# Seven block products for eight in the last up projection of a two-block transformer, with the weight sums on GpSimd

## The reference, cut to what matters

```
D_MODEL = 2048; SEQ = 256; D_FF_2 = 5632
h2 = rmsnorm(x, ffn_norm_g[i])
x = x + (jax.nn.silu(h2 @ w_ffn_gate[i]) * (h2 @ w_ffn_up[i])) @ w_ffn_down[i]
return rmsnorm(x, final_norm_g)
```

## Time and profile before

| | |
|---|---|
| median of 3 runs | 2800.74 us (2800.68 to 2802.15) |
| the profiled execution | 2802.66 us, its span 2800.8 us |
| PE busy | 2784.7 us, 99% of the span |
| VectorE, ScalarE, GpSimd busy | 1947.5, 1377.4, 167.3 us |
| granted TensorE clock, mean | 0.998 |

### The profile page before, as it was taken

One profiled execution on the slowest core, in us unless ns is written; L12 is line 12 of the kernel. 1 busy time (PEld: TensorE's weight loads), 2 busy tenths in 40 slices (PEclk: granted clock), 3 DMA queues, 4 the chain that ended last, 5 costly groups with the idle time before them and its releaser, 6 DMA issues.

```text
span 2800.8 us, 45274 instructions
## 1 busy us (share of the span) xinstructions
PE 2784.7 (99%) x15267; PEld 2385.4 (85%) x15267; DVE 1947.5 (70%) x2978; ACT 1377.4 (49%) x1865; POOL 167.3 (6%) x82
## 2 busy tenths in 40 slices
PE   9999999999999999999999999999999999999998
PEld 7888988888888888888888888888888888888887
DVE  6987787866885786788866777777655555555555
ACT  5336755544554455665544555554454444443444
POOL 6860010000000000000000000000000000000000
PEclk9999999999999999999999999999999999999999
DMA  8975365665665665655555655655666656656664
GB/s 227 260 181 136 92 181 180 192 205 188 188 192 191 187 193 186 186 149 160 154 190 177 181 170 173 182 173 180 196 203 189 190 190 195 188 188 195 189 191 154
DMA packets 510448, 512.69 MB, mean 183 GB/s; under 512 B 90014, under 2 KB 410366, under 8 KB 509822
## 3 DMA queue, kind: packets, MB, share of 16 engines
q1 hardware_dynamic: 510254, 511.19, 60.7%
q10 hardware_dynamic: 80, 0.01, 0.0%
HBM read 505.83 MB, written 5.24 MB: 182 GB/s over the span
## 4 chain that ended last, share of the span: by engine, by line
PE 97%; DVE 1%; SPq 1%; DMA 0%; POOL 0%; ACT 0%; issue 0%; ACTq 0%; DVEq 0%
PE banks L1936 32%; PE banks L1939 16%; PE banks L1968 12%; PE banks L1966 12%; PE banks L1967 12%; PE banks L1951 3%; PE banks L1912 2%; PE banks L1953 1%; SPq L433 1%; PE banks L1920 1%; PE banks L2207 1%; PE banks L1922 1%; PE banks L1921 1%; PE banks L2333 0%; PE banks L2383 0%; PE banks L2016 0%
## 5 line engine op out<-in xcount | busy, mean ns | idle before, releaser
L613 ACT ACTIVATE w_two<-w_raw 128x1024 fp32r<-128x1024 f32 x944 | 995.2, 1059 | 1135.9 <-PE banks L1968 555.1
L1090 DVE TENSOR_TENSOR w_two<-w_raw,w_two 128x1024 fp32r<-128x1024 f32 (+1 forms) x881 | 1075.6, 1229 | 655.3 <-ACT w_two L613 649.3
L1936 PE MATMUL banks<-hp,w_two 128*128 128x512 f32 x3200 | 1012.5, 397 | 1.8 <-issue 1.0
L1939 PEld LDWEIGHTS banks<-hp,w_two 128*128 128x128 f32 x3200 | 601.1, 188 | 140.6
L1939 PE MATMUL banks<-hp,w_two 128*128 128x256 f32 x3200 | 632.0, 278 | 0.0
L1936 PEld LDWEIGHTS banks<-hp,w_two 128*128 128x128 f32 x3200 | 489.3, 189 | 8.9 <-issue 5.1
L1966 PE MATMUL banks<-w_two,yp 128*128 128x512 f32 x1056 | 412.0, 390 | 0.0
L1968 PE MATMUL banks<-w_two,yp 128*128 128x512 f32 x1056 | 411.0, 389 | 0.0
L1967 PE MATMUL banks<-w_two,yp 128*128 128x512 f32 x1056 | 411.0, 389 | 0.0
L1968 PEld LDWEIGHTS banks<-w_two,yp 128*128 128x128 f32 x1056 | 198.2, 188 | 41.4
L1967 PEld LDWEIGHTS banks<-w_two,yp 128*128 128x128 f32 x1056 | 198.3, 188 | 40.6
(11 more groups left out here) (310 smaller groups left out, 2412.0 us busy)
## 6 DMA issues: line engine op xcount, KB each, us to landing
w_raw<-in_w_in SPq DMA_DIRECT2D x480, 256.0 KB, 3.1
w_raw<-in_w_up SPq DMA_DIRECT2D x352, 256.0 KB, 2.9
w_raw<-in_w_down SPq DMA_DIRECT2D x176, 256.0 KB, 3.0
w_raw<-in_w_ffn_gate SPq DMA_DIRECT2D x176, 256.0 KB, 2.8
w_raw<-in_w_ffn_up SPq DMA_DIRECT2D x176, 256.0 KB, 2.9
w_raw<-in_w_ffn_down SPq DMA_DIRECT2D x176, 256.0 KB, 3.3
w_raw<-in_w_out SPq DMA_DIRECT2D x128, 256.0 KB, 3.6
w_raw<-in_w_mla_proj SPq DMA_DIRECT2D x64, 256.0 KB, 3.0
```

What stands on the lines that cost most here:

```text
L613: nc.scalar.activation(w_hi[:, s, 0:n], w_raw[:, s, 0:n], ACT.Copy).then_inc(hi_ready, 1)
L1090: v.tensor_tensor(w_lo[:, s, 0:n], w_raw[:, s, 0:n], w_hi[:, s, 0:n].bitcast(f32), ALU.subtract)\
L1936: mm(banks[:, b, :], w_hi[:, s, at:at + P], rhs[:, k0 + k, :], start=k0 + k == kt_first, stop=False)
L1939: ins = mm(banks[:, b, 0:T], w_lo[:, s, at:at + P], rhs[:, k0 + k, 0:T], start=False, stop=k0 + k == kt_last)
```

## The change

The first step of the last up projection stays as it is (phase `up2_0`, now with one step). The other ten steps become three runs (`run0` to `run2`, of 3, 4 and 3 steps). In a run the input tiles are paired: tile k with tile k + 8. For the pairs 0 to 5 (`QUADS = 6`) the eight block products (two token blocks, two input halves, gate and up) are replaced by seven products of sums, a quad: with gate blocks G0, G1 and up blocks U0, U1 (0 and 1 the input halves), GpSimd forms T1 = U0 - G0, T2 = U1 - T1, T3 = U1 - U0, T4 = G1 - T2 (`sum_1` to `sum_4`), and the activations are used as four prepared sums S1 to S4 and as they are. Pairs 6 and 7 are done plainly (`plain`). A step has 7 x 6 + 8 = 50 operands (`OPS`), each one input tile by 512 columns, and PE does 6 x 7 x 3 + 8 x 2 x 3 = 174 matmuls of 512 columns. Every operand is split in hi by ScalarE (`op_high`) and in lo by VectorE (`op_low`), except four plain ones of each step, which GpSimd splits (`by_pool`). The seven results collect in seven banks; VectorE adds them together into gate and up (`plus`: eight adds a step, each from a bank and an SBUF operand), and ScalarE copies one. The gate and up products (`gate_products`, `mids`: four a step) now read SBUF alone. S1 to S4 are made once, by ten GpSimd adds and four GpSimd subtractions of 128x768 beside four ScalarE copies, while `up2_0` runs. Weights come in blocks of 128x512, as many bytes as before and one DMA of 256 KB each as before, into eleven raw places (three more in `cst`), with eight places for the split operands. The turning of a step's result (`mid_turn`) uses bank 7 and lies after quads 1 and 3 of the next step.

In NSA, unit 1 of `w_out_conv` no longer waits for unit 0 to be taken out, and VectorE does `lo("q", 0, 12)` between `scores(0)` and `scores(1)` rather than behind them.

```diff
+QUADS = 6
+PLAIN = [h + k for h in (0, KT // 2) for k in range(QUADS, KT // 2)]
+T1, T2, T3, B11, B21, B22, T4 = range(7)
+FIRST_PLAIN = 7 * QUADS
+OPS = FIRST_PLAIN + 2 * len(PLAIN)
+BLOCKS = 2 * KT
+RUNS = [(p, 1 if p == 0 else 0, k // 4) for p, (t, k) in enumerate(PARTS)]
+RUN_NAMES = [f"run{p}" for p in range(len(PARTS))]
+S_AT = (3, 5, 8, 10, 14)
+OP_SLOTS, RAW_SLOTS = 2 * R, 2 * R + 3
...
+def by_pool(n):
+    return n % OPS >= FIRST_PLAIN and n % 2 == 1
...
+            for r, (p, i0, i1) in enumerate(RUNS):
+                t0, n = PARTS[p]
+                for st in range(i1 - i0):
+                    cols = slice(t0 * P + (i0 + st) * WIDE, t0 * P + (i0 + st + 1) * WIDE)
+                    for m in range(BLOCKS):
+                        b = BLOCKS * st + m
+                        if m < 4 * QUADS:
+                            g, c = divmod(m, 4)
+                            w, k = (w_gate, w_up, w_up, w_gate)[c], g + c // 2 * (KT // 2)
+                        else:
+                            half, k = divmod(m - 4 * QUADS, len(PLAIN))
+                            w, k = (w_gate, w_up)[half], PLAIN[k]
+                        block_wait(r, b)
+                        sp.dma_start(raw_block(b), w[k * P:(k + 1) * P, cols]).then_inc(block_raw(b), 16)
...
+            def op_high(r, n):
+                src = block_of(n) if n % OPS >= FIRST_PLAIN or n % OPS % 7 in (B11, T3, B22, B21) else None
+                if n % OPS < FIRST_PLAIN and n % OPS % 7 in (T1, T2, T3, T4):
+                    act.wait_ge(sem("op_sums"), sums_made(r, n // OPS * QUADS + n % OPS // 7, n % OPS % 7))
+                else:
+                    act.wait_ge(block_raw(src), block_arrived(r, src))
+                if n >= OP_SLOTS:
+                    act.wait_ge(unit_used, U0[f"run{r}"] + n - OP_SLOTS + 1 + LEAD)
+                else:
+                    act.wait_ge(unit_used, U0[f"run{r}"] - R + n // 2 + 1 + LEAD)
+                nc.scalar.activation(op_hi(n), op_source(n), ACT.Copy).then_inc(hi_ready, 1)
...
+            v1, v2, v3, v4 = (s_f[j][:, :, P:] for j in range(4))
+            added.link(s_step(v1, act_part(0, 1, 0), act_part(1, 1, 0), ALU.add))
+            added.link(s_step(s_tmp, act_part(0, 1, 1), act_part(1, 1, 1), ALU.add))
+            added.link(s_step(v1, v1, s_tmp, ALU.add))
+            added.link(s_step(v2, v1, act_part(0, 0, 0), ALU.subtract))
+            added.link(s_step(v2, v2, act_part(0, 0, 1), ALU.subtract))
...
+            def sum_1(r, q):
+                first, second = came(r, q, 0), came(r, q, 1)
+                if q > 1:
+                    wait_low(pool, r, quad_op(q - 2, T1))
+                nc.gpsimd.tensor_tensor(t_first[:, q % 2, :], second, first, ALU.subtract).then_inc(sem("op_sums"), 1)
+            def sum_2(r, q):
+                last = came(r, q, 2)
+                pool.wait_ge(sem("op_sums"), sums_made(r, q, T1))
+                if q > 1:
+                    wait_low(pool, r, quad_op(q - 2, T4))
+                nc.gpsimd.tensor_tensor(t_other[:, q % 2, :], last, t_first[:, q % 2, :], ALU.subtract).then_inc(sem("op_sums"), 1)
+            def sum_3(r, q):
+                last, second = came(r, q, 2), raw_block(quad_block(q, 1))
+                nc.gpsimd.tensor_tensor(second, last, second, ALU.subtract).then_inc(sem("op_sums"), 1)
+            def sum_4(r, q):
+                third = came(r, q, 3)
+                wait_low(pool, r, quad_op(q, T2))
+                nc.gpsimd.tensor_tensor(t_other[:, q % 2, :], third, t_other[:, q % 2, :], ALU.subtract).then_inc(sem("op_sums"), 1)
+            def plain_low(r, n):
+                if by_pool(n):
+                    pool.wait_ge(hi_ready, U0[f"run{r}"] + n + 1)
+                    nc.gpsimd.tensor_tensor(op_lo(n), op_source(n), op_hi(n).bitcast(f32), ALU.subtract).then_inc(sem("op_low_pool"), 1)
...
+            lo("q", 0, 12)
             scores(1)
-            lo("q", 0, 12)
...
+            def op_low(r, n):
+                if not by_pool(n):
+                    dve.wait_ge(hi_ready, U0[f"run{r}"] + n + 1)
+                    v.tensor_tensor(op_lo(n), op_source(n), op_hi(n).bitcast(f32), ALU.subtract).then_inc(sem("op_low"), 1)
+            def plus(dst, a, bank):
+                return v.tensor_tensor(dst, banks[:, bank, :], a, ALU.add).then_inc(chunk_out, 1)
...
+                down, nu = f"down2_{p}", n // 2
+                r, (_, i0, i1) = p, RUNS[p]
+                for st in range(i1 - i0):
+                    gs, n0 = t0 // 4 + i0 + st, OPS * st
+                    for m in range(6 if st == 0 else 0, OPS):
+                        op_low(r, n0 + m)
+                        if st and m == 2:
+                            gate_sums(r, n0 - len(PLAIN) - 1)
+                        if st and m == 4:
+                            gate_products(gs - 1)
+                        if st and m == 6:
+                            up_sums(gs - 1, r, n0 - 1)
+                        if st and m == 7:
+                            mids(gs - 1)
+                        if m in (21, 35) and i0 + st:
+                            mid_low(gs - 1, i0 + st - 1, m // 35, 7)
+                        if m == FIRST_PLAIN + 3:
+                            common_sums(gs, r, n0 + 7 * (QUADS - 1) + B11)
...
-                    free("w_out_conv", 0, n)
+                    free("w_out_conv", 0, n if n > 1 else 0)
...
+            def product(r, n, g, bank, xh, xl, first, last):
+                wh, wl = op_hi(n), op_lo(n)
+                mm(banks[:, bank, :], xh, wh, start=first, stop=False)
+                mm(banks[:, bank, :], xh, wl, start=False, stop=False)
+                return mm(banks[:, bank, :], xl, wh, start=False, stop=last)
...
+            def quad(r, st, g):
+                operands = (s_tile(1, g), s_tile(2, g), s_tile(3, g), act_tile(0, g, 0), act_tile(1, g, 0), s_tile(4, g), act_tile(1, g, 1))
+                for o, (xh, xl) in enumerate(operands):
+                    n = OPS * st + 7 * g + o
+                    wait_low(pe, r, n)
+                    if g == 0 and st == 0 and o in (T1, T3):
+                        pe.wait_ge(chunk_out, C0[f"run{r}"] - (2 if o == T1 else 0) + LEAD)
+                    if g == 0 and st and o in (T1, B21, B22, T4):
+                        pe.wait_ge(chunk_out, C0[f"run{r}"] + 12 * (st - 1) + {T1: 4, B21: 5, B22: 9, T4: 9}[o] + LEAD)
+                    product(r, n, g, o, xh, xl, g == 0, o in (T1, T2, T3, B11) and g == QUADS - 1).then_inc(unit_used, 1)
...
+                    for g in range(QUADS):
+                        quad(r, st, g)
+                        if g in (1, 3) and i0 + st:
+                            mid_turn(t0 // 4 + i0 + st - 1, g // 2, 7)
+                    for m in range(2 * len(PLAIN)):
+                        if m == len(PLAIN) and i0 + st:
+                            pe.wait_ge(sem("mid"), MID0 + 2 * (t0 // 4 + i0 + st))
+                        plain(r, st, m)
```

More of the change, by code:

```diff
@@ L578, in _ @@
             sp.dma_start(final_row, bass.AP(A["final_norm_g_2"].tensor, 0, [[0, P], [1, D]])).then_inc(loaded["final"], 16)
[L579 to L586, removed]
+            w_gate, w_up = A["w_ffn_gate_2"][0], A["w_ffn_up_2"][0]
@@ L1858, in _ @@
                             lows(down, i, nu + 4, n)
-                            lows(*((down, 1) if i == 0 else (f"up2_{p + 1}", 0)), 0, 4)
+                            if i == 0:
+                                lows(down, 1, 0, 4)
+                            else:
+                                for m in range(6):
+                                    op_low(r + 1, m)
                         used(down, i, nu * (g + 1))
@@ L1862, in _ @@
                             token_residual(c, b, 2 * g + b)
[L1863 to L1864 removed]
+                        if c == 1:
+                            lows(down, 1, 4, 9)
                 else:
@@ L2419, in _, with mid_turn @@
                          (sem("merged_lo"), u // 2 + 1) if c == 0 else None)
-            def mid_turn(i, done):
-                pe.wait_ge(chunk_out, i * 4 + (C0[f"up2_{p}"] + 4 + LEAD))
-                pe.wait_ge(sem("mid"), i * 2 + (MID0 + 2 * done))
-                for t in range(4):
+            def mid_turn(gs, h, bank):
+                if gs == 0:
+                    pe.wait_ge(chunk_out, C0["up2_0"] + 4 + LEAD)
+                else:
+                    pe.wait_ge(chunk_out, sums_done(gs) + 12)
+                if bank == 7 and h == 1:
+                    pe.wait_ge(sem("mid"), MID0 + 2 * gs + 1)
+                for t in (2 * h, 2 * h + 1):
@@ new lines, in plain @@
+            def plain(r, st, m):
+                half, j = divmod(m, len(PLAIN))
+                n, kt = OPS * st + FIRST_PLAIN + m, PLAIN[j]
+                wait_low(pe, r, n)
+                for b, bank in enumerate((B21, T4) if half == 0 else (B22, 7)):
+                    ins = product(r, n, 0, bank, *act_tile(0, kt, b), half == 1 and b == 1 and j == 0, j == len(PLAIN) - 1)
```

(6 more changed lines are left out.)

348 lines of the change are left out of this document (283 added, 65 removed).

## The result

The changed kernel takes 2995.52 us (median of 4 runs, 2994.82 to 2996.79) against 2800.77 before: ratio of the fast runs 1.0692, 95% interval 1.0679 to 1.0706. It is slower by 195 us. The forecast was 2966 with a range of 2905 to 3060.

The account below looks back on a forecast made before the run. PE bound the kernel before; afterwards VectorE and GpSimd taking turns on SBUF would. 597 + 13 + 10 - 21 + 3 + 10 - 3 = 609 us for 444.3, plus 165: 2966 us, range 2905 to 3060.

Parts of the forecast that it names:

- The mechanism: Ten steps: GpSimd and VectorE exclude each other on SBUF, 1.16 us per sum, 0.54 per subtraction; PE waits for lo.
- it does what it says: Rival: the turns are accidental or gaps get filled, PE stays the bound, 2757 us; 8 in 100 including near no change.
- The partial exclusion: Rival: half of VectorE's share hidden, a step 46 us, 2800 + 30, up to 2915; 10 in 100.
- a step of 60 to 64 us: Sign of the forecast: a changed step's length, from one step's turning to the next one's.
- over 100 us of PE waits on L2138: Sign of the forecast: PE's waits in the changed stage released by VectorE's L2138, over 100 us in all.
- The ten steps: Last up projection's rewritten steps: 597 us of turns, with hand-overs, PSUM reads, run ends, start, clock and NSA 609.
- the third: Ten VectorE PSUM-reading instructions a step: mostly beside GpSimd work, 0 to 6.1 us uncovered, taken as 1, 10 in all.
- The ends of the runs: First quad's work made ahead, plain part limited by PE: minus 7 us a run, minus 21 in all (-30 to -9).
- The start: Making S1 to S4 beside up2_0: 43 us in a step of 44.4, uncovered up to 5 us, taken as 3.
- The clock: PE's clock may fall to 1.2 GHz while it waits in quads: 0 to 5 us a step, 10 in all.
- NSA: The 1.89 us PE wait and some slow clock behind it go: 1.9 to 3.6 us faster, taken as 3.
- the upper end: Uncovered PSUM reads 61 us, clock 50, hand-overs 25: ten steps 706 or so, about 3063 us in all.

Follow-up runs that it names:

- the memset run: Changed kernel with each of GpSimd's 240 weight sums replaced by two memsets, same waits and signals, sums' values left out: 2785.72 us, ratio to before 0.9943.
- run 0: Not a follow-up: first of the three stretches of the changed kernel's ten rewritten steps (`run0`), 3 steps, 193.05 us.
- run 2: Not a follow-up: last of the three stretches of the changed kernel's ten rewritten steps (`run2`), 3 steps, 186.37 us.
- three quads on VectorE: Changed kernel with three quads a step for six, all sums and splits on VectorE, second turning moved: 2805.89 us, ratio to before 1.0014.

## Why the prediction was right, and where its sizes were off

- **The mechanism** held in each part: the two engines take turns, 1.69 us for a sum and a subtraction (1.70 forecast), bank operands are free of it, and PE waits for `op_low`. The Trainium skill's page SBUF — State Buffer, section "Who interferes with whom", also says that a GpSimd instruction that only writes does not exclude a VectorE one with two SBUF inputs; the memset run agrees, with 42 us a step for 63. The rival "it does what it says" fell in the trace; the memset run shows about what it would have been worth, 2786 us and not the 2757 put for it. The partial exclusion fell too, since turns have their full length. Two of the signs named beforehand were narrowly missed: a step of 60 to 64 us (65.05), and over 100 us of PE waits on L2138 (95.1).
- **The ten steps** were put at 609 us and are 630.5, which is most of what the forecast fell short. A step in the middle is 65.05 us, where the terms gave 59.7 + 1.3 + 1 + 1 = 63. The term that was too small is the third, 1 us for VectorE instructions that read PSUM while GpSimd has nothing to run beside them. These rows of the step from 2788.74 show VectorE's bank instructions and waits, and behind them GpSimd's idle times:

```profile
2797.81 1.27 DVE L2142 TENSOR_TENSOR arena<-banks,arena 128x512 f32<-128x512 f32 x2
2801.53 2.48 DVE L2138 TENSOR_TENSOR w_two<-w_raw,w_two 128x512 fp32r<-128x512 f32 x4
2805.87 4.49 DVE L2138 TENSOR_TENSOR w_two<-arena,w_two 128x512 fp32r<-128x512 f32 x3 [1.85 <-ACT w_two L1188]
2818.26 0.68 DVE L2194 TENSOR_TENSOR hp<-banks,hp 128x512 fp32r<-128x512 f32 x1
2834.94 0.68 DVE L2194 TENSOR_TENSOR hp<-banks,hp 128x512 fp32r<-128x512 f32 x1
2842.57 2.60 DVE L2142 TENSOR_TENSOR arena<-banks,arena 128x512 f32<-128x512 f32 x4
```

```profile
2801.75 3.42 POOL L1352 TENSOR_TENSOR arena<-w_raw,arena 128x512 f32<-128x512 f32 x1 [5.02 <-DVE w_two L2138]
2819.68 1.60 POOL L1352 TENSOR_TENSOR arena<-w_raw,arena 128x512 f32<-128x512 f32 x1 [2.49 <-DVE w_two L2138]
2836.37 1.61 POOL L1352 TENSOR_TENSOR arena<-cst,arena 128x512 f32<-128x512 f32 x1 [3.10 <-DVE w_two L2138]
2843.83 1.30 POOL L1333 TENSOR_TENSOR arena<-w_raw 128x512 f32<-128x512 f32 x1 [2.34 <-issue]
```

  The two up adds, both `mid_low` and the first two of the four common adds fall while GpSimd is idle: 1.2 + 0.6 + 0.6 + 1.3 = 3.7 us in which neither engine takes a turn, for 1 in the sum. Counting the whole step from the end of each turn to the end of the next gives 59.7 us of turns, 3.9 of uncovered PSUM reads and 1.5 of hand-overs, 65.1 in all; nothing is left for the clock's 1 us. I had taken that GpSimd nearly always has work. Three of its idle times are waits of `sum_4` for the lo of T2. The one of 5.02 us is the longest because that lo stands, at a step's start, behind the up adds and `mids` in VectorE's program; I had looked at this chain within a quad only. But a wait of one engine is no loss while the other works through subtractions that must be done anyway, as VectorE does in most of the 5.02 us, and GpSimd in the 1.85 us for which VectorE waits at 2805.87. The account is read from the trace; moving the adds was not tried.
- **The ends of the runs** were put at 21 us gained and gave 20 (650.5 for ten middle steps, less 630.5), but not 7 each: runs 1 and 2 gained 9 each and run 0 only 2, which belongs to the next point. The right total is luck.
- **The start** was put at 3 us, with a bound of 5, and cost more. GpSimd's fourteen instructions began at 2074.33, 15 us into `up2_0`, whose first matmul is at 2059.01, and were through at 2107.8, 33.5 us for the 26 they take undisturbed. PE's last plain matmul started at 2105.22, its first of the run at 2111.07: 5.85 us where 0.23 is usual, 5.6 lost. The cover was short by the late begin, which I had not looked for: the chain waits until all of `yp` is split. Two more costs follow. About 1.7 us went ahead of that, 1.3 of them a wait for a `lo`. And inside run 0, PE stands once for 6.5 us until L2210, the up product of `up2_0`, gives a bank back (the third of the waiting rows above): it is behind six `op_low` in VectorE's program, and the first of them waits 7.2 us for its operand. Run 0 took 193.05 us, run 2, also of three steps, 186.37. That this wait makes the whole difference was not tested.

```profile
2074.33 4.62 POOL L1297 TENSOR_TENSOR arena<-yp 128x768 f32<-128x768 f32 x2 [889.58 <-DVE yp L1858]
...
2098.75 9.04 POOL L1319 TENSOR_TENSOR arena_r<-arena,arena_r 128x768 fp32r<-128x768 f32 x4
...
2107.76 1.25 POOL L1333 TENSOR_TENSOR arena<-cst 128x512 f32<-128x512 f32 x1
```

- **The clock** granted was 0.94 to 0.97 in the runs. It fell once in each step but the first of a run, where PE had stood 4 to 5 us for the add that gives a bank back, and was up again after 7 to 11 matmuls; it was also low over the first 18 matmuls of run 0 and a few of run 2. At the lower level, 1.2 GHz, matmuls start 0.43 us apart, as below. The 10 us put for it do not show in the account of a step: PE waits for the two engines again a few operands later.

```profile
2863.68 0.77 PE L2833 MATMUL banks<-w_two,arena_r 128*128 128x512 f32 x1 [5.25 <-DVE arena L2142]
2864.24 0.63 PE L2834 MATMUL banks<-w_two,arena_r 128*128 128x512 f32 x1
2864.67 0.63 PE L2835 MATMUL banks<-w_two,arena_r 128*128 128x512 f32 x1
```

- **NSA** was 3 us, and is 3.4 by itself.
- Together, of the 194 us between the two spans: 186.7 more in the ten steps (443.7 before, from first matmul to last), 5.6 + 1.7 at the start, 3.5 back from NSA, and 3.6 in the three stretches behind the runs, where the waits of PE sum to 0.5, 0.5 and 0.8 us; the rest of that is not taken apart.
- **In the prediction's own sums**, the upper end is off: its parts (10 to 61, 10 to 50 and 13 to 25 us) added to 609 make 712, about 3068 us, not 706. The range, which ends at 3060, does not hang on it.

## What to carry to other kernels

Before giving elementwise work to GpSimd, ask how many operands of VectorE's instructions beside it lie in SBUF. If two, and GpSimd's own instruction reads SBUF, the two engines' times added here instead of overlapping, and the work was cheaper on VectorE itself, by 98 us. It costs nothing only where VectorE then still ends before PE does. Ask too what the other engine has to do while one of them does work that is free of the turns: if it is waiting just then, that work is not free. Sum the turns over the shortest stretch that the buffers can smooth (here, it seems, a quad), not over the loop. And a saving of matmuls by an algorithm with sums has to be weighed against the split of each new operand: six quads saved 18 matmuls of 0.227 us a step and added 18 subtractions and 24 sums of 512 columns.

## What was unexpected of the hardware

- The two engines do not always alternate. In seven places `sum_4`, issued at a time when VectorE went from one ready subtraction to the next, stood through three more of them: 3.42 us for what takes 1.29. In the rows above it was issued at 2801.75, VectorE's four subtractions ended at 2804.01, and it ended 1.16 us later, at 2805.17; elsewhere it is let through behind the one that is running. What sets those seven apart stays open.
- A late operand costs PE more than the idle time that the profile shows. With three quads on VectorE a step's 183 matmuls take 0.241 us on the mean (45.01 less 0.87 for turning) for 0.227 before. But most still follow each other at 0.23; some 2 us of the 2.6 lost lie in five operands. Below, the first matmul of one starts 0.63 us behind the one before it, with 0.24 of idle time shown, and the second 0.34 behind the first, 0.5 us lost in all. The idle time is short because it counts from a matmul's end, and matmuls overlap:

```profile
2157.67 0.39 PE L2826 MATMUL banks<-w_two,yp 128*128 128x512 f32 x1
2158.30 0.50 PE L2824 MATMUL banks<-w_two,yp 128*128 128x512 f32 x1 [0.24 <-DVE w_two L2126]
2158.64 0.40 PE L2825 MATMUL banks<-w_two,yp 128*128 128x512 f32 x1
```
